# Causal mask of a stick-breaking attention: as a second matmul into the scores, or as products on VectorE

## What is computed

```python
z = jnp.einsum('bqhd,bkhd->bhqk', q, k) * (SB_HEAD_DIM ** -0.5)
z = z + bias[None, :, None, None]
mask = k_pos[None, :] < q_pos[:, None]
lb = jnp.where(mask, jax.nn.log_sigmoid(-z), 0.0)
rev = lax.cumsum(lb, axis=3, reverse=True)
after = jnp.concatenate([rev[..., 1:], jnp.zeros_like(rev[..., :1])], axis=-1)
wgt = jnp.where(mask, jnp.exp(jax.nn.log_sigmoid(z) + after), 0.0)
out = jnp.einsum('bhqk,bkhd->bqhd', wgt, v)
```

## Time and profile before

| | |
|---|---|
| time, median of 3 runs | 2551.48 us (2548.41 to 2552.57) |
| the profiled execution: its time / its span | 2551.12 us / 2549.4 us |
| granted TensorE clock, mean | 0.952 of full speed |
| PE busy | 2361.7 us, 93% of the span |
| DVE busy | 1364.1 us, 54% |
| ACT busy | 802.0 us, 31% |
| loop over heads, on DVE | about 556 to 730 us from the span's start |

### The profile page before, as it was taken

The page is one execution under the profiler, slowest core; times in us unless marked ns, Lnnn a source line. Parts: engine busy times, 40 slices in busy tenths (PEclk is TensorE's granted clock), DMA queues, the critical chain, the costliest instruction groups (busy, mean ns, idle before and its releaser), DMA issues.

```text
span 2549.4 us, 44080 instructions
## 1 busy us (share of the span) xinstructions
PE 2361.7 (93%) x18353; PEld 2249.2 (88%) x18353; DVE 1364.1 (54%) x1524; ACT 802.0 (31%) x988; POOL 383.8 (15%) x296
## 2 busy tenths in 40 slices
PE   7999999977889999999999998988888878999998
PEld 7999999863369999999999998878788767999997
DVE  4433444778845443445443445677776767443443
ACT  4222222223323222223222223452525344221223
POOL 0000011760011000012000012060514264000000
PEclk8999999977899999999999998989899898999999
DMA  4333326563522323324323323232332322323322
GB/s 136 83 91 96 94 73 191 153 178 101 152 64 70 95 79 103 93 68 114 88 82 100 99 65 93 80 92 79 93 94 75 95 67 77 86 83 111 91 74 75
DMA packets 409348, 244.35 MB, mean 96 GB/s; under 512 B 11106, under 2 KB 386218, under 8 KB 409184
## 3 DMA queue, kind: packets, MB, share of 16 engines
q1 hardware_dynamic: 408791, 242.59, 33.8%
q10 hardware_dynamic: 444, 0.17, 0.0%
HBM read 228.81 MB, written 14.58 MB: 95 GB/s over the span
## 4 chain that ended last, share of the span: by engine, by line
PE 75%; DVE 13%; POOL 4%; ACT 4%; issue 2%; DMA 0%; SPq 0%; ACTq 0%; POOLq 0%; DVEq 0%
PE PS L220 69%; DVE cbuf L1221 3%; POOL prod L875 3%; PE PS L1069 2%; DVE xcs L2000 1%; DVE wl L197 1%; PE PS L1782 1%; DVE xcs L2167 1%; DVE cdec L2178 1%; ACT wh L193 1%; PE PS L1699 1%; DVE dec L2174 0%; DVE spl L1320 0%; ACT dec L1886 0%; DVE spl L1327 0%
## 5 line engine op out<-in xcount | busy, mean ns | idle before, releaser
L220 PE MATMUL PS<-hh,wh 128*128 128x260 f32 x3792 | 777.5, 286 | 27.4 <-DVEq L637 7.9
L220 PE MATMUL PS<-hh,wl 128*128 128x260 f32 x3792 | 770.4, 285 | 0.0
L220 PE MATMUL PS<-hl,wh 128*128 128x260 f32 x3792 | 770.0, 285 | 0.0
L220 PEld LDWEIGHTS PS<-hh,wh 128*128 128x128 f32 x3792 | 591.8, 191 | 39.6 <-issue 23.5
L220 PEld LDWEIGHTS PS<-hh,wl 128*128 128x128 f32 x3792 | 590.3, 190 | 0.4
L220 PEld LDWEIGHTS PS<-hl,wh 128*128 128x128 f32 x3792 | 590.1, 190 | 0.5
L197 DVE TENSOR_TENSOR wl<-raw,wh 128x2048 fp32r<-128x2048 f32 (+2 forms) x194 | 442.4, 2281 | 203.5 <-ACT wh L193 203.0
L193 ACT ACTIVATE wh<-raw 128x2048 fp32r<-128x2048 f32 (+2 forms) x194 | 352.5, 1817 | 317.2 <-PE PS L220 284.1
L220 PE MATMUL PS<-hid_l,wh 128*128 128x260 f32 x1408 | 283.8, 283 | 0.0
L220 PE MATMUL PS<-hid_h,wh 128*128 128x260 f32 x1408 | 283.2, 282 | 0.0
L220 PE MATMUL PS<-hid_h,wl 128*128 128x260 f32 x1408 | 283.0, 282 | 0.0
(11 more groups left out here) (299 smaller groups left out, 2395.6 us busy)
## 6 DMA issues: line engine op xcount, KB each, us to landing
raw<-in_ffn_gate_dram SPq DMA_DIRECT2D x88, 512.0 KB, 4.0
raw<-in_ffn_up_dram SPq DMA_DIRECT2D x88, 512.0 KB, 5.2
raw<-in_ffn_down_dram SPq DMA_DIRECT2D x64, 384.0 KB, 4.0
raw<-in_ffn_down_dram SPq DMA_DIRECT2D x64, 320.0 KB, 3.6
raw<-in_m_in_proj_dram SPq DMA_DIRECT2D x40, 512.0 KB, 5.2
page<-in_cache_sb_v_dram SPq DMA_DIRECT2D x48, 256.0 KB, 3.0
raw<-in_ab_in_proj_dram SPq DMA_DIRECT2D x20, 512.0 KB, 5.3
ms_b<-in_state_ssm_dram SPq DMA_DIRECT2D x32, 256.0 KB, 3.0
```

What stands on the lines that cost most here:

```text
L220: ins = pe.matmul(out, x[:, k0, c:c + m], y[:, k, half * H2:(half + 1) * H2], start=k == 0 and a == 0, stop=k == nk - 1 and a == 2)
```

## The change

The mask becomes part of the scores. `later` holds 0 where the query comes after the key and -2^100 elsewhere; behind each of the four matmuls of `scores` a matmul of the identity with `later` adds it to the diagonal block in PSUM. A masked score then has softplus 0 and weight 0 by itself. Both calls of `diagonal` on DVE go, and PE waits for `sp_max` and `w_exp` where it waited for `sp_done` and `w_mask`.

```diff
-                qmask = sb_in(st, "qmask", [P, P])
+                later = sb_in(st, "later", [P, P])
...
-                    pool.memset(qmask[:, :], 1.0).then_inc(S["masks"], 1)
+                    pool.memset(later[:, :], 0.0).then_inc(S["masks"], 1)
...
-                    pool.affine_select(out=qmask[:, :], in_=qmask[:, :], compare_op=ALU.is_ge, fill=0.0, base=-1,
+                    pool.affine_select(out=later[:, :], in_=later[:, :], compare_op=ALU.is_ge, fill=-FAR, base=-1,
                                        pattern=[[1, P]], channel_multiplier=-1).then_inc(S["masks"], 1)
...
                         for kb in range(NTT):
-                            ins = pe.matmul(z_ps[:, KO[kb]:KO[kb] + KW[kb]],
-                                            kT[r:r + DH, h // 2, kb * P:(kb + 1) * P],
-                                            qT[r:r + DH, h // 2, kb * P:T], start=True, stop=True)
+                            pe.matmul(z_ps[:, KO[kb]:KO[kb] + KW[kb]],
+                                      kT[r:r + DH, h // 2, kb * P:(kb + 1) * P],
+                                      qT[r:r + DH, h // 2, kb * P:T], start=True, stop=False)
+                            ins = pe.matmul(z_ps[:, KO[kb]:KO[kb] + P], ident[:, :], later[:, :],
+                                            start=False, stop=True)
...
+                    pe.wait_ge(S["masks"], 5)
                     scores(0)
                     v_tokens(2)
                     v_tokens(3)
-                    pe.wait_ge(S["masks"], 5)
...
-                            pe.wait_ge(S["w_mask"], h + 1)
+                            pe.wait_ge(S["w_exp"], h + 1)
...
-                            pe.wait_ge(S["sp_done"], h + 1)
+                            pe.wait_ge(S["sp_max"], h + 1)
...
-                    def diagonal(a):
-
-                        ms = qmask[:, :].rearrange("p (a c) -> p a c", a=1).to_broadcast([P, 2, P])
-                        for t in (a[:, 0:KO[2]].rearrange("p (a c) -> p a c", a=2)[:, :, 0:P],
-                                  a[:, KO[3]:KO[3] + 2 * P].rearrange("p (a c) -> p a c", a=2)):
-                            ins = dve.tensor_tensor(t, t, ms, ALU.mult)
-                        return ins
...
-                            dve.wait_ge(S["sp_max"], i + 1)
-                            diagonal(s).then_inc(S["sp_done"], 1)
...
-                            dve.wait_ge(S["w_exp"], i)
-                            diagonal(sp_[:, (i - 1) % NSP, :]).then_inc(S["w_mask"], 1)
```

More of the change, by code:

```diff
@@ L720, in stage_a @@
             QS, ES, KS = 2, 3, 10
+            FAR = 2.0 ** 100
             with ExitStack() as st:
@@ L764, in stage_a @@
                          "val0 val1 val2 val3 val4 val5 val6 val7 prod_done prod_free z_mm abs_done e_done lnp_done z_cp sp_max "
-                         "sp_done sum_mm t_done w_exp w_mask pv_mm pv_hi pv_lo dscore dabs de dlnp dsf_done dsum_mm "
+                         "sum_mm t_done w_exp pv_mm pv_hi pv_lo dscore dabs de dlnp dsf_done dsum_mm "
                          "dt_done dw_exp dpv_mm orow_cp orow_zero os_tr os_hi mix_lo").split()
@@ L1342, in on_dve @@
                             ins.then_inc(S["dsf_done"], 1)
-                        if 1 <= i <= NH:
-                            dve.wait_ge(S["w_exp"], i)
-                            diagonal(sp_[:, (i - 1) % NSP, :]).then_inc(S["w_mask"], 1)
                         if i == 2:
```

## The result

The changed kernel took 2560.72 us (median of 7 runs, 2558.80 to 2566.49), the kernel before 2549.97 on the same chips (7 runs, 2547.16 to 2552.57): a ratio of 1.0048, 95% interval 1.0037 to 1.0059. By the medians it is slower by 10.7 us, by the ratio by 12.2 (9.4 to 15.0), and it lies outside the range of the prediction, which said 2553.0 and 2546 to 2558. One run of a later experiment (the changed kernel with the sums moved) took 3828 us at a mean granted clock of 0.55 and is left out there.

What follows compares the result with a forecast made beforehand. PE's matmuls bound the whole span, with PE and DVE nearly balanced in the head loop. Round terms 1.7 - 1.4 + 1.0 + 0 + 0 + 0.7 + 0.9 - 1.2 = +1.7 on 2551.12 led to 2553.0 us, range 2546 to 2558.

Steps and rivals of the forecast that it cites:

- the price of the change of rows: In scores on PE, seven more switches per head between 64-row and 128-row matmuls: 0.1 us each, 0.7 per head.
- x: Fixed part of a head's score matmul time on PE, independent of columns and clock: 0.28 us, upper bound per switch.
- the moment of the clock's rise: PE's clock was taken to rise at 577.2, near 638.6 and near 679.6 in rounds 0, 3 and 5.
- The prediction's own range: Total time 2548 to 2556 us, from no price for changes of mode to a clock that rises late.
- The rule of the Trainium skill: Masks alternating with 64-row matmuls change tiling mode, which drains TensorE; not charged by its words, as no row isolates it.
- The changes of mode are dear: Rival, slower: at 0.28 us each, a head's masks cost 3.7 slow, 2.8 fast; sum +9.9, 2561 us; chance 0.17.
- The removal: Mask products leave DVE, 1.43 us per round; gains where DVE sets the pace, none in rounds 2 and 4.
- The balance of PE and DVE: In the head loop, both nearly balanced: PE's sums ready 1.4 us before DVE in round 3, 0.6 in round 5.
- the first rival: Clock stays up: masks leave PE less idle, scores and masks take 4.0 us; sum -5.4, 2545.7 us; chance 0.1.

Runs made afterwards that it cites:

- the 64-row run: Changed kernel with each mask matmul taking only 64 rows of identity and mask, so half the mask is left out: 2547.73 us, ratio 0.9995 to the kernel before.
- the run with one-pass masks: Changed kernel with a head's four masks in one group and identity and mask held as fp32r copies: 2546.52 us, ratio 0.9993 to the kernel before.

## Why the prediction was wrong

*The step that failed* is the price of the change of rows: "So it costs between 0 and 0.28 each, 0 to 2.0 per head. I take 0.1 each, a third of x, as x pays two things: 0.7." Both things that x paid, 0.16 to begin and 0.13 to end, are paid again at every change. It measured 0.30 slow and 0.20 fast, at the end of the bound that I had worked out, and a head's masks 3.8 and 2.3 us. The term was mis-sized threefold at the low clock and twofold at the high one; the 64-row run shows it as the cause, since without the changes, and with all else but the masks' full depth, the loss of 10.7 us is gone. The bound itself came out right by luck: it set a start-to-start time (4.56) beside a duration (2.42) and took x as the same at both clocks. With 2.35 in place of 2.42 the same sum gives x = 0.14, half of what a change cost at the low clock.

*A second step that failed* is the moment of the clock's rise. The prediction let it come when it had come before (577.2, 638.6 and 679.6). In the changed kernel the stretch from 577.2 to 582 was still at 0.50, the two sums of round 2 took 3.7 us until DVE had them (620.90 to 624.56; forecast 1.8), and the value products of rounds 3 and 5 took 4.15 and 4.53, nearly all or all of it slow. This made rounds 0, 2, 3 and 5 some 2 us each dearer than even the dear price had them. The prediction's own range reckoned with a late rise, but only to 2556.

*The rule of the Trainium skill* (page TensorEngine Tiling, section Tiling Modes: changing the tiling mode, not just the tile, drains TensorE) stood against the change in the prediction, and the runs agree that the change costs: 0.29 us at a granted clock of 0.50 and 0.20 at 1.00 for each, none with 64-row masks. That this time is a drain, no run here shows.

*The rival "The changes of mode are dear"* was the right one, and its sign is there (a set of 8.34 us where it was slow, over 7.5). That its sum of +9.9 (2561) is only 0.3 us off the measured time is partly luck: the loop lost 13.5, not 9.9. Rounds 0, 2, 3 and 5 lost 5.5, 4.1, 3.2 and 4.0 where it said 3.6, 2.4, 1.3 and 1.9; round 6 lost nothing (2.2) and round 7 gained 2.7 (1.2). The clock took and gave these differences, as told above and below. By the medians the stages behind the loop gave back 2.8. I gave it 0.17.

*The removal*: right in the sum and in which rounds could gain, not in their sizes. 6.4 us of the loop were gained without masks, but round 3 gave 0.3 and round 6 2.25, by the clock. Rounds 2 and 4 gave nothing (round 2 lost 0.6), round 4 with the hole of 1.39 us ahead of L197 that the prediction named.

*The balance of PE and DVE*: right, and the reason why the price mattered at once. PE became the bound of rounds 3, 5 and 6, as stated, and of round 1 too (a wait of 0.99 us), where the prediction had left PE 0.2 us and had DVE never idle.

*The clock*: the first rival's mechanism exists, but not where it was looked for. Rounds 2, 3 and 5 began their scores slow, after 3.01, 4.49 and 6.78 us of idle PE. Rounds 6 and 7 had their value product at the high level throughout (2.37 and 2.34 us, against 3.91 and 3.75): in round 6 this paid for the dear masks (0 instead of +0.9), in round 7 it doubled the gain.

## What to carry to other kernels

An operation that moves to TensorE is priced by its columns and by what it does to its neighbours: here matmuls of another depth between 64-row matmuls cost a change on either side. Collecting them behind one another took most of that price away; giving them the same rows took all of it, in a run that leaves out half of the mask. Where a residue in the trace may pay for the start, the end, or both, and the edit repeats it eight times a head, forecast with the whole residue, or keep the chance of that end as high as the middle. And where two engines are within 1 us of each other, the same edit can be worth 6.4 or 2.6 us, so put the work that someone waits for (here the sums of the samples) ahead of the part that grows. A forecast that moves work on PE must also move the moment at which the clock rises.

## What was not expected of the hardware

A one-pass fp32r matmul of 128 columns behind its like took 0.19 us at the low clock and 0.10 at the high one ((694.66 - 694.07 - 0.20) / 4, granted clock 1.00), about half of what an fp32 one takes (0.43 and 0.21) and not a quarter; no run shows why. The rows at the high clock, from the run with one-pass masks:

```profile
694.07 0.66 PE L972 MATMUL PS<-later_r,ident_r 128*128 128x128 f32 x4
694.66 0.49 PE L968 MATMUL PS<-qT,kT 64*128 64x128 f32 x2
```

And moving two sums ahead of the scores was worth 11.7 us to the changed kernel, 4.5 of them in round 3, which the move doesn't touch: with 0.70 us of idle PE ahead of them the scores of that round ran at the high level, where after 4.49 us they had run at the low one.
